# NSA's local probabilities turned in 32x32 blocks by VectorE and regrouped through DRAM, in a Trainium2 decoder block

## What is computed

```python
h = rmsnorm(x, norm_mix_g)
z = h @ w_in + b_in
(ga, gb, gc, fq, fk, fv, ff, cb, cc, cx,
 nq, nkc, nvc, nks, nvs, nkw, nvw, ng) = split(z)
y_a = fox_attention(fq, fk, fv, ff) @ w_br_a        # 8 heads of 64, forget bias
y_b = (cb * causal_dwconv(cc * cx, sc_conv_w)) @ w_br_b
y_c = nsa_attention(nq, nkc, nvc, nks, nvs, nkw, nvw, ng, ...) @ w_br_c
mix = sigmoid(ga) * y_a + sigmoid(gb) * y_b + sigmoid(gc) * y_c
x = x + mix @ w_o
u, v = split(rmsnorm(x, norm_ffn_g) @ w_up)
x = x + (silu(causal_dwconv(u)) * v) @ w_down
return rmsnorm(x, norm_final_g)

# nsa_attention, per query head (8 heads, 2 key/value groups):
o = g0 * compressed(q) + g1 * selected(q) + g2 * local(q)
# compressed: 31 keys, made by a small MLP from overlapping blocks of 32 tokens
# selected:   the top 16 blocks of 64 tokens; there are 8, so all are taken
# local:      a window of 512 tokens, so all causal keys
```

## Time and profile before

| | |
|---|---|
| median of 3 runs | 900.0 us (899.93 to 900.48) |
| the profiled execution | 900.83 us |
| its span, first to last instruction | 899.0 us |
| PE (TensorE matmul) busy | 885.9 us, 99% |
| VectorE (DVE) busy | 518.8 us, 58% |
| GpSimd (POOL) busy | 381.8 us, 42% |
| ScalarE (ACT) busy | 379.5 us, 42% |
| chain of waits: PE's share | 82% |
| DMA, mean over the span | 113 GB/s |

### The profile page before, as it was taken

One profiled execution on the slowest core, in us unless ns is written; L12 is line 12 of the kernel. 1 busy time (PEld: TensorE's weight loads), 2 busy tenths in 40 slices (PEclk: granted clock), 3 DMA queues, 4 the chain that ended last, 5 costly groups with the idle time before them and its releaser, 6 DMA issues.

```text
span 899.0 us, 13389 instructions
## 1 busy us (share of the span) xinstructions
PE 885.9 (99%) x4266; PEld 737.8 (82%) x4266; DVE 518.8 (58%) x1041; ACT 379.5 (42%) x651; POOL 381.8 (42%) x198
## 2 busy tenths in 40 slices
PE   8999999998999999999999999999999999999997
PEld 7888888787888888888888888888888888888886
DVE  5537566578565855757658886666666666401102
ACT  6445454454453554445434444333333333311125
POOL 4454445543234333334233674444444444444441
PEclk9999999997999999999999999999999999999999
DMA  6356574764122322212256334554443333322232
GB/s 194 105 138 171 150 216 128 195 177 101 48 71 71 94 58 82 71 47 82 59 119 149 106 96 116 129 127 117 136 144 93 94 99 109 118 94 94 94 117 93
DMA packets 184979, 101.25 MB, mean 113 GB/s; under 512 B 55135, under 2 KB 174317, under 8 KB 184949
## 3 DMA queue, kind: packets, MB, share of 16 engines
q1 hardware_dynamic: 184517, 100.08, 40.4%
q10 hardware_dynamic: 432, 0.79, 0.2%
HBM read 91.38 MB, written 9.45 MB: 112 GB/s over the span
## 4 chain that ended last, share of the span: by engine, by line
PE 82%; issue 8%; POOL 5%; DMA 2%; DVE 2%; ACT 1%; SPq 1%; POOLq 0%; ACTq 0%; DVEq 0%
PE z_bank L717 20%; PE z_bank L719 20%; PE z_bank L718 20%; POOL w_lo L623 4%; PE s_bank L719 3%; PE s_bank L717 3%; PE s_bank L718 3%; PE s_bank L756 2%; PE s_bank L784 2%; PE s_bank L914 1%; DMA x_in<-in_x 1%; PE s_bank L799 1%; POOL f_diag L669 1%; PE s_bank L808 1%; PE o_bank L808 1%
## 5 line engine op out<-in xcount | busy, mean ns | idle before, releaser
L623 POOL TENSOR_TENSOR w_lo<-raw,w_hi 128x1024 fp32r<-128x1024 f32 (+1 forms) x143 | 344.3, 2407 | 498.1 <-ACT w_hi L1049 421.0
L717 PE MATMUL z_bank<-h_hi,w_hi 128*128 128x512 f32 x752 | 295.7, 393 | 0.5 <-POOL w_lo L623 0.4
L719 PE MATMUL z_bank<-h_hi,w_lo 128*128 128x512 f32 x752 | 293.4, 390 | 0.0
L718 PE MATMUL z_bank<-h_lo,w_hi 128*128 128x512 f32 x752 | 293.3, 390 | 0.0
L1049 ACT ACTIVATE w_hi<-raw 128x1024 fp32r<-128x1024 f32 x116 | 122.3, 1054 | 173.2 <-PE z_bank L719 168.4
L717 PEld LDWEIGHTS z_bank<-h_hi,w_hi 128*128 128x128 f32 x752 | 141.6, 188 | 31.0 <-POOL w_lo L623 1.5
L719 PEld LDWEIGHTS z_bank<-h_hi,w_lo 128*128 128x128 f32 x752 | 141.4, 188 | 29.9
L718 PEld LDWEIGHTS z_bank<-h_lo,w_hi 128*128 128x128 f32 x752 | 141.7, 188 | 28.5
L1741 DVE SCALAR_TENSOR_TENSOR u_c<-u_t,cols,u_c 128x512 f32<-128x512 f32 x44 | 64.7, 1471 | 25.1 <-ACT u_c L1296 22.1
L1058 ACT ACTIVATE p_f<-p_f,neg_mx 128x128 f32<-128x128 f32 (+1 forms) x96 | 52.7, 550 | 41.5 <-DVE neg_mx L1591 27.1
L1750 DVE TENSOR_TENSOR act_lo<-u_c,act_hi 128x512 f32 (+1 forms) x22 | 40.8, 1854 | 19.8 <-ACT act_hi L1302 19.8
(11 more groups left out here) (366 smaller groups left out, 1309.9 us busy)
## 6 DMA issues: line engine op xcount, KB each, us to landing
raw<-in_w_in SPq DMA_DIRECT2D x112, 256.0 KB, 3.2
raw<-in_w_up SPq DMA_DIRECT2D x88, 256.0 KB, 3.2
raw<-in_w_down SPq DMA_DIRECT2D x42, 256.0 KB, 2.9
p_scratch<-p_t SPq DMA_DIRECT2D x8, 640.0 KB, 4.2
p_d<-p_scratch SPq DMA_DIRECT2D x32, 160.0 KB, 4.0
raw<-in_w_o SPq DMA_DIRECT2D x16, 256.0 KB, 3.2
...
```

The lines of the kernel that those rows point to most:

```text
L623: pool.tensor_tensor(w_lo[:, slot, 0:wide], raw[:, slot, 0:wide], w_hi[:, slot, 0:wide].bitcast(F), ALU.subtract) \
L717: pe.matmul(out, w[0], r[0], start=first, stop=False, skip_group_check=onto)
L718: pe.matmul(out, w[0], r[1], start=False, stop=False, skip_group_check=onto)
L719: return pe.matmul(out, w[1], r[0], start=False, stop=last, skip_group_check=onto)
```

## The change

The local branch's probabilities take FoX's way. VectorE turns each head's tile in 32x32 blocks right behind its normalisation; SP stores and reloads it (store_turned, load_keys); PE has no transposes there and runs the query projection of the next pair (weight n+8) between gate C's projection and the local product. ScalarE's query work of the next pair (nsa_q) comes ahead of its work behind the product, and VectorE's q_lo moves from the head of a pair to its end. The last pair takes the first gate C step of the mix ("gc", 6) in the place of a query projection, and MIX_ORDER puts both gate steps first. The selected branch keeps its PE transposes. Besides, `group_rows(0)` moves from the end of the last FoX pair to its start, ahead of VectorE's scores, and in SP's FoX list the load of weight n+2 goes ahead of the wait for the masked scores and of the load of f_bias. `p_d` and `o_t` get other places in SBUF. The diff, without the moved text of group_rows, the tiles' places and renamed arguments:

```diff
-MIX_ORDER = (("gc", 6), ("yc", 0), ("yc", 2), ("gc", 7), ("yc", 4), ("yc", 6))
+MIX_ORDER = (("gc", 6), ("gc", 7), ("yc", 0), ("yc", 2), ("yc", 4), ("yc", 6))
...
+            def store_turned(turn):
+                for a in range(2):
+                    sp.wait_ge(p_turned, 2 * turn + a + 1)
+                    sp.dma_start(p_dram[a], p_t[:, a, :]).then_inc(p_stored[a], 16)
+
+            def load_keys(turn):
+                for a in range(2):
+                    sp.wait_ge(p_stored[a], 16 * turn + 16)
+                    for kj in range(P128 // BLK):
+                        sp.dma_start(p_d[BLK * kj:BLK * kj + BLK, a, :].rearrange("p (b c) -> p b c", b=P128 // BLK),
+                                     p_dram[a].rearrange("(b k) (j c) -> j k b c", b=P128 // BLK, j=P128 // BLK)[kj]) \
+                            .then_inc(p_landed[a], 16)
...
+                load8(n + 2, 1, w_k, O_CB + P128 * i)
                 sp.wait_ge(masked, i + 1)
                 sp.dma_start(f_bias[:, :, :], cum_dram[ds(2 * i, 2), :].rearrange("(o h) n -> o h n", o=1)
                              .to_broadcast([P128, 2, SEQ])).then_inc(fbias_loaded, 16)
-                load8(n + 2, 1, w_k, O_CB + P128 * i)
...
+                store_turned(i)
+                load_keys(i)
...
-            with sp.Fori(0, PAIRS) as i:
+            def nsa_loads(i, first):
                 n = N_NSA + 8 * i
                 load_nq(n, 1, i)
+                if not first:
+                    store_turned(PAIRS + i - 1)
                 load8(n + 1, 0, w_k, O_GA + 2 * P128 * i)
+                if not first:
+                    load_keys(PAIRS + i - 1)
                 load8(n + 2, 1, w_k, O_GB + 2 * P128 * i)
                 load_ab(n + 3, 0, 2 * i)
                 load8(n + 4, 1, w_k, O_GA + P128 + 2 * P128 * i)
                 load8(n + 5, 0, w_k, O_GB + P128 + 2 * P128 * i)
                 load_ab(n + 6, 1, 2 * i + 1)
                 load8(n + 7, 0, w_k, O_GC + P128 * i)
+
+            nsa_loads(0, True)
+            with sp.Fori(1, PAIRS) as i:
+                nsa_loads(i, False)
...
+                if step == MIX_ORDER[0]:
+                    store_turned(2 * PAIRS - 1)
+                if step == MIX_ORDER[1]:
+                    load_keys(2 * PAIRS - 1)
...
-            def nsa_pair(i, first):
+            assert N_MIX == N_NSA + 8 * PAIRS and Z_MIX[0] == Z_NSA[0] + 5 * PAIRS and N_MIX % 2 == 1
+
+            def nsa_pair(i):
                 n, z = N_NSA + 8 * i, 5 * i
                 z0, z1 = Z_NSA[0] + z, Z_NSA[1] + z
-                if not first:
-                    project(1, 0, n, z0)
                 project(0, 1, n + 1, z1)
...
-                transposes(PAIRS + 2 * i + 1)
                 project(0, 1, n + 7, z1 + 4)
+                project(1, 0, n + 8, z0 + 5)
                 product(vn[:, 1, :, :, :], PAIRS + 2 * i + 1, (False, True), (True, True)).then_inc(pv_done, 1)
-            nsa_pair(0, True)
-            with pe.Fori(1, PAIRS) as i:
-                nsa_pair(i, False)
-
-            n, tau = N_MIX, 0
-            for kind, m in MIX_ORDER:
+            with pe.Fori(0, PAIRS) as i:
+                nsa_pair(i)
+
+            n, tau = N_MIX + 1, 1
+            for kind, m in MIX_ORDER[1:]:
...
-            def fox_pt_high(i):
+            def turned_high(turn):
                 for b in range(5):
-                    act.wait_ge(p_landed[FOX_PARTS[b][0]], 64 * i + 64)
+                    act.wait_ge(p_landed[FOX_PARTS[b][0]], 64 * turn + 64)
                     act.activation(by_query(pt_hi, b), landed(b), ACT.Copy).then_inc(pt_hi_done, 1)
...
-                if not first:
-                    split_hi_in_loop(0, L + 2, T)
-                    nsa_q(i)
...
-                pt_high(PAIRS + 2 * i + 1)
                 act.wait_ge(tile_done, T + 10)
                 tanh_gate(g_c[:, i, :], 1, ds(16 + i, 1))
+                if last:
+                    split_hi((N_MIX + 1) % 2, N_MIX + 1, T_MIX)
+                    turned_high(PAIRS + i)
+                    gate_c(MIX_ORDER[0][1], 0, T_MIX + 1)
+                else:
+                    split_hi_in_loop(0, L + 6, T + 10)
+                    turned_high(PAIRS + i)
+                    nsa_q(i + 1)
...
+            def turned_low(pair):
                 for b in range(5):
-                    dve.wait_ge(pt_hi_done, 5 * i + b + 1)
+                    dve.wait_ge(pt_hi_done, 5 * pair + b + 1)
...
+                if last:
+                    dve.wait_ge(z_free[1], Z_CMP[1] - 2)
+                    group_rows(0, C_PEK, cols1)
...
                 else:
-                    dve.wait_ge(z_free[1], Z_CMP[1])
-                    group_rows(0, C_PEK, cols1)
                     group_rows(1, C_PEV, cols2)
...
-                dve.wait_ge(q_hi_done, PAIRS + i + 1)
-                sub_lo(q_lo[:, :], Z[0][:, :], cols1[:, ds(C_NQ + i, 1)], q_hi[:, :], z_free[0])
                 softmax_scores(PAIRS + 2 * i, score_at)
...
                 for a in range(2):
                     gated_norm(PAIRS + 2 * i + 1, 2, a)
+                    turn_blocks(PAIRS + 2 * i + 1, a)
                 gated_a(2 * i + 1, T + 7, z1 + 3)
                 gated_b(2 * i + 1, T + 7, z1 + 3, z0 + 4)
-                pt_low(PAIRS + 2 * i + 1)
+                turned_low(PAIRS + 2 * i + 1)
+                if not last:
+                    nsa_q_lo(i + 1)
```

More of the change, by code:

```diff
@@ L219, in hybrid_block @@
         vc = sb("vc", [P128, 2, P128], R, att)
+        with ExitStack() as s:
+            o_t = sb("o_t", [P128, SEQ], F, s)
         cz = sb("cz", [P128, 2, HALF_R, CZ_W], F, att)
@@ L259, in hybrid_block @@
             o_s = sb("o_s", [P128, SEQ], F, s)
-            o_t = sb("o_t", [P128, SEQ], F, s)
+        with ExitStack() as s:
+            pad_both = sb("pad_both", [P128, 13928], F, s)
+            p_d = sb("p_d", [P128, 2, P_ALL], F, s)
         att.close()
@@ L1154, in fox_pair @@
                 act.activation(br_hi[:, PAIRS + i, :], conv_c[:, :], ACT.Copy).then_inc(conv_hi, 1)
-                fox_pt_high(i)
+                turned_high(i)
                 if last:
@@ L1197, in _, with nsa_pair @@
                 act.activation(vc[:, a, 0:64], O[:, cols], ACT.Copy).then_inc(cmp_hi, 1)
-            def nsa_pair(i, first):
+            def nsa_pair(i, last):
                 T, L = T_NSA + 10 * i, 4 * i + N_NSA // 2
                 z0, z1 = Z_NSA[0] + 5 * i, Z_NSA[1] + 5 * i
-                if not first:
-                    split_hi_in_loop(0, L + 2, T)
-                    nsa_q(i)
                 def tanh_gate(dst, z, col):
@@ L1222, in nsa_pair @@
                 split_hi_in_loop(0, L + 4, T + 5)
-                pt_high(PAIRS + 2 * i)
+                pt_high(i)
                 act.wait_ge(c_ready, i + 1)
@@ L1245, in nsa_pair @@
                 act.activation(c_hi[64:P128, i, :], o_t[64:P128, :], ACT.Copy).then_inc(o_hi_done, 1)
-            nsa_pair(0, True)
-            with act.Fori(1, PAIRS) as i:
+            with act.Fori(0, PAIRS - 1) as i:
                 nsa_pair(i, False)
+            nsa_pair(PAIRS - 1, True)
             def mix_high(m):
@@ L1257, in _ @@
             for kind, m in MIX_ORDER:
-                split_hi((n + 1) % 2, n + 1, T_MIX + tau)
+                if n > N_MIX:
+                    split_hi((n + 1) % 2, n + 1, T_MIX + tau)
                 for mt in pending:
@@ L1261, in _ @@
                 pending = []
-                if kind == "gc":
+                if n == N_MIX:
+                    tau += 1
+                elif kind == "gc":
                     gate_c(m, tau % 2, T_MIX + tau + 1)
@@ L1360, in turn_blocks, with pt_low @@
                 dve.transpose(to[:, 7, :, :], part[:, 3, :, :]).then_inc(p_turned, 1)
-            def pt_low(pair):
+            def pt_low(pair, i):
                 for b in range(5):
@@ L1365, in pt_low @@
                     if b == 0:
-                        dve.wait_ge(pt_ready, 5 * pair + 5 - 5 * PAIRS)
+                        dve.wait_ge(pt_ready, 5 * i + 5)
                     dst, src = pt_part(pt_lo, b)
@@ L1480, in fox_q_lo, with group_rows @@
                 sub_lo(q_lo[:, :], Z[0][:, :], cols1[:, ds(C_FQ + i, 1)], q_hi[:, :], z_free[0])
+            def group_rows(b, pe_col, pe_cols):
+                for s in range(2):
+                    to = slice(64 * s, 64 * s + 64)
+                    for g in range(2):
+                        rows = slice(64 * g, 64 * g + 64)
+                        hi, lo = (t[rows, b, :].bitcast(F).rearrange("p (c s r) -> p s r c", s=2, r=HALF_R)[:, s, :, :] for t in (nk_hi, nk_lo))
+                        dve.tensor_tensor(cz[to, b, :, N_BLK * g:N_BLK * g + N_BLK], hi, lo, ALU.add).then_inc(cz_ready, 1)
+                    dve.tensor_copy(cz[to, b, :, 2 * N_BLK:CZ_W],
+                                    pe_cols[0:64, pe_col:pe_col + CMP_LEN].rearrange("p (h s r) -> p s r h", h=2, s=2)[:, s, :, :]) \
+                        .then_inc(cz_ready, 1)
             def fox_k_lo(i):
```

(19 more changed lines are left out.)

23 lines of the change are left out of this document (6 added, 17 removed).

## The result

The changed kernel takes 920.33 us (median of 4 runs, 918.84 to 921.45) where the kernel before took 899.96 on the same chip: a ratio of 1.0222, interval 1.021 to 1.0234. That is 20.4 us slower; the forecast was 10.9 slower and a range up to 919.

What follows compares the result with a forecast made beforehand. PE was taken to bound the kernel, busy 885.9 of 899.0 us. The terms 12.2 - 3.3 - 0.9 + 0.9 + 2 = +10.9 gave 911.7 against 900.83, so a 910.9 us median; range 899.5 to 919.

Steps and rivals of the forecast that it cites:

- the clock's term: PE's clock behind the four NSA waits: 1.3 us per fall, in some of the places; +2 us (bounds 0, 20).
- the block sums: Half the block sums go ahead of the last FoX pair's scores, shortening PE's wait: -3.3 us (bounds -5.4 and -1.7).
- the earlier load: FoX weight load before f_bias removes the 0.40 us wait of FoX pair 3 with its restart: -0.9 us (bounds -1, 0).
- What goes: In each NSA pair, 20 PE transposes before the gate projection go, 2.10 us; four times, -8.4 us.
- VectorE's turns and the small product: NSA pairs: two 1.75 us turns and a 128x4 product held by GpSimd's split idle PE +3.84 us per pair.
- Rival B: NSA pairs: only the small product slips through, the lows are held; +0.85 per pair, 900.1 us, chance 0.09.
- Rival E: NSA pairs: head 1's normalise meets GpSimd's split of 332.19 too; +2 a pair, 919 us, chance 0.08.
- Rival A: NSA pairs: neither the small product nor the lows are held; -0.4 per pair, 895.1 us, chance 0.10.
- The round trip: Head 1's keys via DRAM, back at 344.1 to 345, hidden behind lows held by GpSimd; +3.05 us per pair, +12.2 for four.
- Rival C: The clock falls in all four NSA waits for 10 us: +20 for the +2, 929 us, chance 0.08.
- a shorter wait before the block sums: Sign of a right forecast: PE waits 2.6 us in place of 3.16 at the block sums.
- Mix: Eight output tiles in a row; the fifth tile's gating comes after PE wants its bank: +0.9 us (bounds 0 and 3).

Runs made afterwards that it cites:

- m1_narrow: The changed kernel with one GpSimd weight split per NSA pair (gate C's) cut to 8 of 1024 columns: 911.61 us, 1.0125 times before.
- m5_keys_first: The order of m3_norms_first, with each head's eight key loads ahead of gate A's weight load in SP's list: 935.16 us, 1.0387 times before.
- m3_norms_first: The changed kernel with both heads normalised before either is turned, branch A's gating between the turns: 916.91 us, 1.0194 times before.
- m2_gate_first: The changed kernel with the gating of branch A moved ahead of head 1's softmax: 924.57 us, 1.0275 times before.
- m6_no_trip: The order of m3_norms_first without the stores and key loads of the four local branches, local output not from its own probabilities: 898.38 us, 0.998 times before.
- m4_keep_clock: The changed kernel with 30 spare transposes in the wait before gate C's projection of each NSA pair: 920.68 us, 1.0211 times before.
- p5_mix: The kernel before with only the mix's second gate C projection moved ahead of the first w_br_c step: 901.43 us, 1.0018 times before.

## Why the prediction was wrong

The sign and the mechanism of the pairs were right, the size was half of the truth, and 920.33 lies 1.3 us above the range. The steps that failed are the clock's term, put at 2.0 us where 5.8 came, and the block sums and the earlier load, put at -4.2 where -1.1 came. Step by step:

- *What goes*: right, -8.4.
- *VectorE's turns and the small product*: right. Product 2.37 us (forecast 2.34), PE idle 3.61, 3.61, 3.61 and 3.48. The forecast's 3.84 counts from 330.86, but the branch's last matmul ended at 331.02, so that its own times give 3.68. m1_narrow shows the cause. Rival B, in which the product slips through and the pair gains, is wrong by pair 4: it slipped through, and the next instruction was held as long. Rival E needed the second split for this; it was the first. Rival A's product would be out at 346.6, not 345.95, by the tail of 1.56 that the forecast itself uses; its time would be 897.5, not 895.1.
- *The round trip*: right in size, and in what decides by luck. The held lows were to give +3.05 a pair. With the clock's loss of 2.7, 1.5, 0 and 1.6 us that makes 5.8, 4.5, 3.1 and 4.7; the traces have 5.7, 4.4, 3.7 and 4.3. The excess in pair 3 is the keys'. These were put at 10.1 to 11 us and took 12.1 to 13.5; in pairs 2 and 4 they would have decided if the slow clock had not made the held lows some 1.5 us late as well. What the 10.1 of FoX lacked was not traffic, since its DMA engines were as full, but the weight load between stores and key loads: "344.1 to 345" allows up to 0.9 us for it, and m5_keys_first against m3_norms_first has 2.1 to 2.4. That two paths are nearly equal was said ("1 us more"), but not that removing the first would then gain nothing; m2_gate_first and m6_no_trip show it.
- *Clock*, +2: too small, 5.8 in the profiled run. What failed was reading as "Here wide ones follow at once, so 1.3 us": behind three of these waits it stayed at half for 3.1 to 5.8 us under wide matmuls. Rival C, four falls of 10 us, was too much. m4_keep_clock adds that this is not to be had back singly.
- *Block sums sooner*, -3.3 (the 0.5 included), *and the earlier load*, -0.9: in the profiled runs the first gate A projection starts 1.1 sooner, at 228.25 for 229.37, and even this is mostly the recorded run of before being 0.9 above its median: p5_mix, with the same program up to there, has 228.46. Alone, the sums have the wrong sign and cost 1.9 us; the load gives 0.2, which can't be told from nothing. The step that failed was "GpSimd has splits and casts there, so I let them end 1.5 us behind the first score, and allow 0.5": only the sums themselves were held against GpSimd's timeline, not the softmax that they push back. The sign "a shorter wait before the block sums" did not come either: 3.36 us for 3.16.
- *Mix*, +0.9: 1.5 alone, and 1.2 from the last pair to the end of the profiled runs.
- *The profiled run against the median*: before, it was 0.9 above the median; after, 918.84 was the fastest of four and 1.5 below. These 2.4 us are variation from run to run: the granted clock was 0.988 in this run and 0.984 in the three others, of 919.57 to 921.45.
- *The aside on transposes*: the figures of the Trainium skill (VectorE: DVE Perf Modes, "The three transpose paths") are for bf16 tiles, and the tiles here are float32.

From the forecast +10.9 to +20.4, in the profiled run's terms: pairs 3.8 more, as much as the clock's term was short of (18.0 for 14.2 with the clock: 18.2 in the four stretches, 0.2 less in the rest of the pairs), block sums and load 3.1, mix 0.3, profile against median 2.4; 9.6 together, for the 9.5 that are missing.
